# Attention probabilities turned by VectorE in blocks of 32 and by DMA through DRAM, in place of TensorE

## Chip, cores and metric

The kernel runs on one core of a Trainium2 chip. The time is that of the device for one execution, in microseconds (us). TensorE, VectorE (DVE), ScalarE (ACT), GpSimd (POOL) and SyncE (SP) are the core's engines; SyncE only issues transfers here.

## The reference

Two blocks run one after the other over 512 tokens of width 1024. The first (a pooling mixer and a gated recurrent mixer) is not touched by the change. The second has two layers, each with sliding-window attention beside a chunked gating branch:

```python
for l in range(DEPTH):                       # 2 layers
    h = x @ w_in[l] + b_in[l]
    q, k, v, z_a, u_g, v_g, z_g, g_a, g_g = split_columns(h)
    y_a = sliding_window_attention(q, k, v, sinks[l]) * silu(z_a)   # 8 query heads, 2 key heads, width 64
    y_g = chunked_spatial_gating(gelu(u_g), gelu(v_g), ...) * silu(z_g)
    merged = sigmoid(g_a) * (y_a @ w_branch_attn[l]) + sigmoid(g_g) * (y_g @ w_branch_gmlp[l])
    x = layer_norm(ALPHA * x + merged @ w_out[l] + b_out[l], ln_g[l], ln_b[l])
```

The attention works on blocks of 128 queries, each with the block of 128 keys before it and its own (256 keys), with a sink in the denominator:

```python
scores = q . k / 8 - slope * dist, masked to 0 <= dist < 128
m = max(scores, sink);  p = exp(scores - m);  denom = sum(p) + exp(sink - m)
out = (p / denom) @ v
```

## The kernel before

Products with weights are made in three terms (high x high, high x low, low x high) of float32 split into a high part, rounded, and a low one. Weights come from DRAM in loads of 1 MB (`load_chunk`, two buffers), each of which holds two pieces. The high part of a piece is made by ScalarE or, in the stretch of the attention, by a cast of VectorE (`c_split`, L2533), the low part by GpSimd (`split_lo`, L404). A load may be issued when the low part of the last piece in its buffer is done. A piece is split three units ahead of its use (`AHEAD = 3`).

TensorE runs through the units of a layer in a fixed order: q (4 units), k, v, za (4), u (4), vg (4 quarters), zg (4), ga (4), gg (4), then the branch products bra and brg, then a second half of these, then the output. A unit takes 24 products of 512 columns, some 6 us. Between the units stand small pieces of side work in an order that is written out by hand (`C_ORDER`): the attention is cut in 16 blocks, (pair of heads p, query block b) with p from 0 to 3 and b from 0 to 3, and one step of it follows each unit from za 1 on. With b = 0 there is no block of keys before, so half of the work falls away.

Step s on each engine, before the change:

- TensorE (`att_tensor`): for s = 6, 10, 14, 18 the products with the values of four blocks (one pair), into the second bank of `aux2`; then the scores of block s into `aux`; then the transpositions of the probabilities of block s - 2, two or four of 128x128, into the first bank of `aux2`.
- VectorE (`att_gate`, `att_vector`, `att_vector_out`): the gate of a pair when its products with the values are done; the scaling of the probabilities of block s - 1 (L2450); the mask and the row maximum of block s (L2460, L2465). After that it casts the next piece of weights.
- ScalarE (`att_scalar`): the copy of the turned probabilities of block s - 2 from PSUM to `pt` (four buffers, L1828), then the exponentials of block s (L1837), then the high part of a gated pair.

So step s = 7 follows the first quarter of vg, step 12 follows zg 1, step 15 ga 0, steps 16, 17 and 18 ga 1, 2 and 3. The gating branch's own side work (`mix`) follows gg 0 to gg 3. The branch products bra need all four gated pairs.

The first block of the model already turns an operand by VectorE's transposition in blocks of 32 (L2184) and a way through DRAM: SyncE writes `v_turn` (L950) and reads it back in four transfers (L958).

SyncE issues all weight loads of a layer in order, with nothing between them until two small loads near the layer's end. In a layer, load n holds pieces 2n and 2n + 1: load 7 and 8 are vg, 9 and 10 zg, 11 and 12 ga, 13 and 14 gg, 15 bra, 16 brg.

Of the kernel before, what the change touches and what calls it, by code (L numbers as in the profile page):

```python
# [28 lines left out]
F32 = mybir.dt.float32  # L29
F32R = mybir.dt.float32r  # L30
I32 = mybir.dt.int32
ALU = mybir.AluOpType
# [3 lines left out]
P = 128  # L36
# [3 lines left out]
SEQ = 512  # L40
# [97 lines left out]
def program(nc, a, out):  # L138
    with ExitStack() as ctx:
# [126 lines left out]
        with ExitStack() as before_g:  # L266
            ws = sb("ws", [P, 4, P], where=before_g)
            qs_b = sb("qs_b", [P, 4, SEQ], F32R, where=before_g)
            with ExitStack() as in_rows:
                brow = sb("brow", [P, D], where=in_rows)  # L270
            pt_more = [sb(f"pt{s}", [P, 4, P], where=before_g) for s in (2, 3)]
        gac = sb("gac", [P, 4, SEQ], where=in_c)
        ggc = sb("ggc", [P, 4, SEQ], where=in_c)

# [10 lines left out]
        with ExitStack() as before_m:  # L285
            kf = sb("kf", [P, SEQ], where=before_m)
            vf = sb("vf", [P, SEQ], where=before_m)
            vtc = sb("vtc", [P, CH, P], where=before_m)
            sc = [sb(f"sc{s}", [P, 2, 2 * P + 1], where=before_m) for s in range(2)]
            pr = [sb(f"pr{s}", [P, 2, 2 * P + 1], where=before_m) for s in range(2)]  # L290
            pt = [sb(f"pt{s}", [P, 4, P], where=before_m) for s in range(2)] + pt_more
            sgc = [xn[0][:, 0:SEQ], rstd[:, 0:SEQ]]
        with ExitStack() as after_m:
            mlo = sb("mlo", [P, KT, SEQ], F32R, where=after_m)
        in_c.close()
        qs = [(qs_a, qs_b)[n // 4][:, n % 4, :] for n in range(8)]
        qf = [s[:, :, :].rearrange("p x k -> p (x k)")[:, 0:SEQ] for s in sc]
        lng = sqs[:, :, :].rearrange("p s t -> p (s t)")[:, 0:D]
        lnb = xns[:, :, :].rearrange("p s t -> p (s t)")[:, 0:D]
# [55 lines left out]
        apt_full, apt_ready, ao_full = sem("apt_full"), sem("apt_ready"), sem("ao_full")  # L355
        ya_ready, yahi_ready, yalo_ready = sem("ya_ready"), sem("yahi_ready"), sem("yalo_ready")
        vgb_ready, vgg_ready, vgn, vgr_ready = (sem("vgb_ready"), sem("vgg_ready"), sem("vgn"),
                                                sem("vgr_ready"))
# [444 lines left out]
            return LC + C_STEPS * i  # L803

        ATT = [(p, b) for p in range(4) for b in range(CH)]
        STEP_OF = {}
        FREED = {}
        n_steps = 0
# [22 lines left out]
        def c_slots():  # L831

            att = 0
            order = []
            for entry in C_PLAN:
                stage, index, kind, m, half, u = entry
                for q in range(4 if kind == "vg" else 1):
                    side = []
                    if stage == "za" and index == 0:
                        side.append(("vtc", 0))  # L840
                        side.append(("ws", 0))
                    elif att < len(ATT) and stage in ("za", "u", "vg", "zg", "ga", "gg"):
                        side.append(("att", att))
                        att += 1
                    elif att < len(ATT) + 3 and att >= len(ATT):
                        side.append(("att", att))
                        att += 1
                    if stage in ("gg",) and index < 4:
                        side.append(("mix", index))
                    order.append((entry, q, side))  # L850
            return order
# [35 lines left out]
        def _(sp):  # L887
# [115 lines left out]
            for i in range(DEPTH):  # L1003
# [17 lines left out]
                for n, (kind, src) in enumerate(chunks):  # L1021
# [84 lines left out]
        def _(pe):  # L1106
# [272 lines left out]

            def att_tensor(i, s):  # L1380
                base = 16 * i
                for t in range(s - 6, s - 2) if s >= 6 and s % 4 == 2 else ():

                    p, b = ATT[t]
                    pe.wait_ge(apt_ready, 1 + base + t + 1)
                    if b == 0:
                        pe.wait_ge(ya_ready, 1 + 4 * i + p)
                    for kb_ in range(0 if b else 1, 2):
                        for x in range(2):
                            kv = (2 * p + x) // 4  # L1390
                            mm = pe.matmul(aux2[HD * x:HD * x + HD, 1, P * b:P * b + P],  # L1391
                                           vtc[:, b - 1 + kb_, HD * kv:HD * kv + HD],
                                           pt[t % 4][:, 2 * x + kb_, :],
                                           start=(kb_ == (0 if b else 1)), stop=(kb_ == 1))
                    mm.then_inc(ao_full, 1)
                if s < len(ATT):
# [16 lines left out]
                if 2 <= s < len(ATT) + 2:  # L1413

                    t = s - 2
                    b = ATT[t][1]
                    pe.wait_ge(aprob, 3 * (base + t) + 3)
                    pe.wait_ge(apt_ready, 1 + base + t)
                    for x in range(2):
                        for kb_ in range(0 if b else 1, 2):  # L1420
                            mm = pe.transpose(aux2[:, 0, P * (2 * x + kb_):P * (2 * x + kb_ + 1)],  # L1421
                                              pr[t % 2][:, x, P * kb_:P * kb_ + P], ident[:, :])
                    mm.then_inc(apt_full, 1)

            def side_tensor(i, what, n):
                if what == "vtc":
# [141 lines left out]

        @block.scalar
        def _(act):  # L1570
            act.sem_inc(apt_ready, 1)
# [245 lines left out]

            def att_scalar(i, s, between=None):
                base = 16 * i
                if 2 <= s < len(ATT) + 2:  # L1820
                    t = s - 2
                    z, first = t % 2, (0 if ATT[t][1] else 1)
                    act.wait_ge(apt_full, base + t + 1)
                    if t >= 4:
                        act.wait_ge(ao_full, base + t - 3)
                    if t == 2:
                        act.wait_ge(res_ready, 4 * i + 4)
                    act.activation(pt[t % 4][:, :, :].rearrange("p (x k) q -> p x k q", x=2)[:, :, first:, :],  # L1828
                                   aux2[:, 0, :].rearrange("p (x k q) -> p x k q", x=2, k=2)[:, :, first:, :],
                                   ACT.Copy).then_inc(apt_ready, 1)  # L1830
                if between is not None:
                    between()
                if s < len(ATT):
                    lo, z = (0 if ATT[s][1] else P), s % 2
                    act.wait_ge(arow, base + s + 1)
                    for x in range(2):
                        act.activation(pr[z][:, x, lo:], sc[z][:, x, lo:], ACT.Exp,  # L1837
                                       bias=sm[z][:, 0, x:x + 1], accum_out=sm[z][:, 1, x:x + 1])\
                           .then_inc(aexp, 1)
                if s >= 3 and ATT[s - 3][1] == CH - 1:  # L1840
                    p = ATT[s - 3][0]
                    act.wait_ge(ya_ready, 1 + 4 * i + p + 1)
                    act.activation(yah[:, p, :], sq[p % 2][:, 0:SEQ], ACT.Copy).then_inc(yahi_ready, 1)

            for i in range(DEPTH):
                def bias(col):
# [107 lines left out]
        def _(dve):  # L1954
# [486 lines left out]
            def att_vector(i, s):  # L2441
# [10 lines left out]
                if s < len(ATT):  # L2452
# [10 lines left out]
                    dve.wait_ge(asc_ready, 1 + 2 * (base + s) + 2)  # L2463
                    dve.wait_ge(sink_ready, 8 * i + 2 * p + min(b, 1) + 1)
                    dve.tensor_reduce(sm[z][:, 0, :], sc[z][:, :, lo:], AX_X, ALU.max, negate=True).then_inc(arow, 1)  # L2465

            def att_gate(i, s):
                if s >= 3 and ATT[s - 3][1] == CH - 1:
                    p = ATT[s - 3][0]
                    dve.wait_ge(ao_full, 16 * i + s - 2)  # L2470
                    dve.tensor_tensor(sq[p % 2][:, 0:SEQ], aux2[:, 1, :], za[:, p, :], ALU.mult)\
                       .then_inc(ya_ready, 1)

            def att_vector_out(i, s):
                if s >= 3 and ATT[s - 3][1] == CH - 1:
                    p = ATT[s - 3][0]
                    dve.wait_ge(yahi_ready, 4 * i + p + 1)
                    dve.tensor_tensor(yal[:, p, :], sq[p % 2][:, 0:SEQ], yah[:, p, :], ALU.subtract)\
                       .then_inc(yalo_ready, 1)

            def mix_vector(i, g):
# [194 lines left out]
```

## Time and profile before

| | |
|---|---|
| time, median of 3 runs | 1551.97 us (1551.46 to 1552.41) |
| the profiled execution | 1552.21 us, its span 1550.5 us |
| TensorE busy | 1540.2 us, 99% |
| VectorE busy | 1005.7 us, 65% |
| ScalarE busy | 592.1 us, 38% |
| GpSimd busy | 356.5 us, 23% |
| granted clock of TensorE, mean | 0.999 |
| moved by DMA | 149.78 MB, 97 GB/s |

A busy share is over the whole span; products of TensorE are pipelined, so that their durations overlap and the distance of their starts tells the pace. The attention of the first layer lies between 942 and 1062 us, that of the second between 1267 and 1387 us. A queue row (SPq) is an issue of a transfer; its time to landing is counted from the issue to the semaphore.

### The profile page before, as it was taken

How to read it: one execution, taken by the hardware profiler on the slowest of the kernel's cores; microseconds unless marked ns; L12 is line 12 of the kernel's file. 1: busy time of each engine (PE TensorE's matmuls, PEld its weight loads, DVE VectorE, ACT ScalarE, POOL GpSimd, SP SyncE). 2: the span in 40 equal slices, each digit the busy share in tenths (PEclk: the TensorE clock that was granted, in tenths of full speed). 3: DMA queues.
4: the chain of work that ended last, by engine and by line, in shares of the span. 5: the costliest groups of instructions: out<-in, count | busy, mean ns of one | idle time of the engine just before them, and what ended most of it. 6: DMA issues, size and time to landing. Idle time of an engine off the chain costs nothing.

```text
span 1550.5 us, 29971 instructions
## 1 busy us (share of the span) xinstructions
PE 1540.2 (99%) x12487; PEld 1381.8 (89%) x12487; DVE 1005.7 (65%) x1654; ACT 592.1 (38%) x1070; POOL 356.5 (23%) x333
## 2 busy tenths in 40 slices
PE   9999999999999999999999999999999999999998
PEld 9999999999999899899998898888888988888886
DVE  6656565775877678586786677567516786576346
ACT  5323232253444344334444445482112346541121
POOL 0000000020421214042142124334530043343510
PEclk9999999999999999999999999999999999999999
DMA  5322322323332523423243142222324322222331
GB/s 170 110 82 91 101 82 82 110 82 96 105 103 64 134 59 111 119 75 95 72 112 125 55 135 91 75 80 93 97 82 143 122 82 82 82 82 82 117 128 55
DMA packets 124722, 149.78 MB, mean 97 GB/s; under 512 B 4812, under 2 KB 100464, under 8 KB 124592
## 3 DMA queue, kind: packets, MB, share of 16 engines
q1 hardware_dynamic: 120880, 143.17, 30.1%
q10 hardware_dynamic: 3632, 4.53, 0.9%
q8 instruction: 100, 1.64, 0.4%
q0 software_dynamic: 80, 0.20, 0.1%
q14 instruction: 30, 0.25, 0.1%
HBM read 141.33 MB, written 6.55 MB: 95 GB/s over the span
## 4 chain that ended last, share of the span: by engine, by line
PE 98%; DVE 1%; DMA 0%; issue 0%; ACT 0%; SPq 0%; POOL 0%; ACTq 0%; DVEq 0%; POOLq 0%
PE acc L409 28%; PE acc L411 28%; PE acc L410 28%; PE aux L569 1%; PE aux L409 1%; PE aux L411 1%; PE aux L410 1%; PE aux L629 1%; PE aux L631 1%; PE aux L1391 1%; PE aux L1421 1%; PE aux L621 1%; PE aux L550 1%; PE aux L1410 1%; PE aux L1411 0%; PE aux L1445 0%
## 5 line engine op out<-in xcount | busy, mean ns | idle before, releaser
L409 PE MATMUL acc<-xhis,whi 128*128 128x264 f32 (+2 forms) x1848 | 611.3, 331 | 0.0
L411 PE MATMUL acc<-xhis,wlo 128*128 128x264 f32 (+2 forms) x1848 | 602.1, 326 | 0.0
L410 PE MATMUL acc<-xlos,whi 128*128 128x264 f32 (+2 forms) x1848 | 601.8, 326 | 0.0
L411 PEld LDWEIGHTS acc<-xhis,wlo 128*128 128x128 f32 x1848 | 347.9, 188 | 29.2
L409 PEld LDWEIGHTS acc<-xhis,whi 128*128 128x128 f32 x1848 | 348.0, 188 | 28.9 <-issue 0.3
L410 PEld LDWEIGHTS acc<-xlos,whi 128*128 128x128 f32 x1848 | 348.3, 188 | 26.8
L404 POOL TENSOR_TENSOR wlo<-raw,whi 128x1024 fp32r<-128x1024 f32 x84 | 207.7, 2473 | 377.0 <-DVE whi L2533 377.0
L400 ACT ACTIVATE whi<-raw 128x1024 fp32r<-128x1024 f32 x158 | 164.1, 1048 | 133.4 <-PE acc L411 119.2
L404 DVE TENSOR_TENSOR wlo<-raw,whi 128x1024 fp32r<-128x1024 f32 x81 | 99.8, 1235 | 36.9 <-ACT whi L400 36.7
L2230 DVE TENSOR_TENSOR wlo<-raw,whi 128x1024 fp32r<-128x1024 f32 x77 | 93.7, 1218 | 21.9 <-ACT whi L400 21.7
L2533 DVE CAST whi<-raw 128x1024 fp32r<-128x1024 f32 x84 | 66.8, 797 | 54.0 <-PE acc L411 53.8
L1082 POOL TENSOR_TENSOR kb<-kb,fb 128x264 f32<-128x264 f32 x16 | 17.3, 1100 | 285.9 <-PE aux L550 285.9
L1052 POOL TENSOR_TENSOR xns<-sqs 128x528 f32<-128x528 f32 x1 | 1.5, 1454 | 324.0 <-ACT sqs L1679 324.0
L409 PE MATMUL acc<-zhis,whi 128*128 128x264 f32 x256 | 73.2, 286 | 0.0
L411 PE MATMUL acc<-zhis,wlo 128*128 128x264 f32 x256 | 72.7, 284 | 0.0
L410 PE MATMUL acc<-zlos,whi 128*128 128x264 f32 x256 | 72.6, 284 | 0.0
L409 PEld LDWEIGHTS acc<-zhis,whi 128*128 128x128 f32 x256 | 48.2, 188 | 0.6
L410 PEld LDWEIGHTS acc<-zlos,whi 128*128 128x128 f32 x256 | 48.3, 189 | 0.0
L411 PEld LDWEIGHTS acc<-zhis,wlo 128*128 128x128 f32 x256 | 48.2, 188 | 0.0
L2134 DVE TENSOR_TENSOR h<-acc,h 128x528 f32<-128x528 f32 x32 | 22.6, 707 | 38.4 <-PE acc L411 38.4
L1072 POOL TENSOR_TENSOR tb<-tb 128x132 f32<-128x132 f32 (+5 forms) x96 | 38.9, 431 | 0.0
L1837 ACT ACTIVATE pr<-sc,sm 128x257 f32<-128x257 f32 (+1 forms) x64 | 30.4, 478 | 19.8 <-DVE sm L2465 19.7
(390 smaller groups left out, 2781.0 us busy)
## 6 DMA issues: line engine op xcount, KB each, us to landing
raw<-in_w_in SPq DMA_DIRECT2D x38, 1024.0 KB, 5.3
raw<-in_hgrn_w_in SPq DMA_DIRECT2D x32, 1024.0 KB, 6.4
raw<-in_pool_w_in SPq DMA_DIRECT2D x15, 1024.0 KB, 5.5
raw<-in_pool_w_out SPq DMA_DIRECT2D x8, 1024.0 KB, 5.1
raw<-in_hgrn_w_out SPq DMA_DIRECT2D x8, 1024.0 KB, 5.3
raw<-in_w_out SPq DMA_DIRECT2D x8, 1024.0 KB, 5.1
v_turn<-vb SPq DMA_DIRECT2D x8, 544.0 KB, 7.6
raw<-in_pool_w_grp SPq DMA_DIRECT2D x4, 1024.0 KB, 5.2
```

The costliest lines, as they stand in the source:

```text
L400: act.activation(piece(whi, kind, m), raw_view(kind, m), ACT.Copy).then_inc(hi_ready, 1)
L404: dve.tensor_tensor(piece(wlo, kind, m), raw_view(kind, m), piece(whi, kind, m), ALU.subtract).then_inc(lo_ready, 1)
L409: pe.matmul(dst, stat[0], mov[0], start=first, stop=False)
L410: pe.matmul(dst, stat[0], mov[1], start=False, stop=False)
L411: return pe.matmul(dst, stat[1], mov[0], start=False, stop=last)
L550: mm = pe.matmul(first_bank(c, x)[rows, :, col:col + 32], kb[par][x][:, META + t0:META + t0 + 32], both[:, :, t0:t0 + 32], start=True, sto ...
L1072: pool.tensor_tensor(tb[x][2 * m][:, 0:both.shape[1]], both[:, :, 0], both[:, :, 1], ALU.mult)\
L1082: pool.tensor_tensor(first_halves(dst, m), first_halves(src, m), both[:, :, 1].unsqueeze(2).to_broadcast([P, both.shape[1], m]), ALU.mult)\
L1837: act.activation(pr[z][:, x, lo:], sc[z][:, x, lo:], ACT.Exp, bias=sm[z][:, 0, x:x + 1], accum_out=sm[z][:, 1, x:x + 1])\
L2134: dve.tensor_tensor(halves(h[:, n, :]), acc_all(slot), halves(h[:, n, :]), ALU.add)\
L2230: dve.tensor_tensor(piece(wlo, kind, m), raw_view(kind, m), piece(whi, kind, m), ALU.subtract).then_inc(lo_ready, 1)
L2533: dve.tensor_copy(piece(whi, kind, M), raw_view(kind, M)).then_inc(hi_ready, 1)
```

## The change

The probabilities are no longer turned by TensorE and copied by ScalarE. In step t + 1, VectorE transposes the scaled probabilities of block t in blocks of 32x32, two instructions, into `pb` (two buffers, which lie in `sq[1]` and `xn[1]`). SyncE writes `pb` to a DRAM tensor `p_turn` (256 KB), and reads it back in four transfers of 32 partitions (64 KB each), which puts the blocks in their turned places, in `pt`. The places of these transfers among the weight loads in SyncE's order are given by numbers. The products with the values move from steps 6, 10, 14, 18 to 8, 12, 16, 19, and wait once a pair, for the transfers of all four blocks. The attention runs to step 19 (after gg 0). The gated pair is always in `sq[0]`. ScalarE's exponential waits for the transposition of the block two before.

```diff
+        VALUES_AT = {8: 0, 12: 1, 16: 2, 19: 3}
+        p_turn = nc.dram_tensor("p_turn", (len(ATT), P, SEQ), F32).ap()
...
-                    elif att < len(ATT) + 3 and att >= len(ATT):
+                    elif att <= max(VALUES_AT) and att >= len(ATT):
...
+                def probabilities_out(t):
+                    sp.wait_ge(pb_ready, 2 * (16 * i + t) + 2)
+                    sp.dma_start(p_turn[t], pb[t % 2].rearrange("p b n j -> p (b n j)")).then_inc(pb_sent[t % 2], 16)
+
+                def probabilities_in(t):
+                    sp.wait_ge(pb_sent[t % 2], 16 * ((16 * i + t) // 2) + 16)
+                    if t == 2:
+                        sp.wait_ge(res_ready, 4 * i + 4)
+                    if 16 * i + t >= 4:
+                        sp.wait_ge(ao_full, 16 * i + 4 * (t // 4))
+                    blocks = p_turn[t].rearrange("(a p) n -> p a n", a=4)
+                    for b in range(4):
+                        sp.dma_start(pt[t % 4][32 * b:32 * b + 32, :, :, :].rearrange("p a n j -> p a (n j)"),
+                                     blocks[:, :, P * b:P * b + P]).then_inc(pt_landed, 16)
+
+                queue = [(2 * n - 12.5, "load", n) for n in range(len(chunks))]
+                queue += [(t + 2.5, "out", t) for t in range(len(ATT))]
+                queue += [(max(t + 3.3, 4 * (t // 4) + 4.3 + 0.1 * (t % 4) if t >= 4 else 0), "in", t)
+                          for t in range(len(ATT))]
+                for _, what, n in sorted(queue):
...
-                for t in range(s - 6, s - 2) if s >= 6 and s % 4 == 2 else ():
+                for t in range(4 * VALUES_AT[s], 4 * VALUES_AT[s] + 4) if s in VALUES_AT else ():
-                    pe.wait_ge(apt_ready, 1 + base + t + 1)
+                    if b == 0:
+                        pe.wait_ge(pt_landed, 64 * (base + t + 4))
...
-                    for x in range(2):
-                        for kb_ in range(0 if b else 1, 2):
-                            mm = pe.transpose(aux2[:, 0, P * (2 * x + kb_):P * (2 * x + kb_ + 1)],
-                                              pr[t % 2][:, x, P * kb_:P * kb_ + P], ident[:, :])
-                    mm.then_inc(apt_full, 1)
...
-                    act.activation(pt[t % 4][:, :, :].rearrange("p (x k) q -> p x k q", x=2)[:, :, first:, :],
-                                   aux2[:, 0, :].rearrange("p (x k q) -> p x k q", x=2, k=2)[:, :, first:, :],
-                                   ACT.Copy).then_inc(apt_ready, 1)
...
+                    if base + s >= 2:
+                        act.wait_ge(pb_ready, 2 * (base + s - 1))
...
+                if 1 <= s < len(ATT) + 1:
+                    t = s - 1
+                    first, z = (0 if ATT[t][1] else 1), t % 2
+                    dve.wait_ge(aprob, 3 * (base + t) + 3)
+                    if base + t >= 2:
+                        dve.wait_ge(pb_sent[z], 16 * ((base + t) // 2))
+                    for x in range(2):
+                        dve.transpose(pb[z][:, :, 2 * x + first:2 * x + 2, :].rearrange("p b k j -> p k b j"),
+                                      pr[z][:, x, P * first:2 * P].rearrange("p (k b j) -> p k b j", b=4, j=32))\
+                           .then_inc(pb_ready, 1)
...
-                if s >= 3 and ATT[s - 3][1] == CH - 1:
-                    p = ATT[s - 3][0]
-                    dve.wait_ge(ao_full, 16 * i + s - 2)
-                    dve.tensor_tensor(sq[p % 2][:, 0:SEQ], aux2[:, 1, :], za[:, p, :], ALU.mult)\
+                if s in VALUES_AT:
+                    p = VALUES_AT[s]
+                    dve.wait_ge(ao_full, 16 * i + 4 * p + 4)
+                    if 4 * i + p:
+                        dve.wait_ge(yahi_ready, 4 * i + p)
+                        dve.wait_ge(yalo_ready, 4 * i + p)
+                    dve.tensor_tensor(sq[0][:, 0:SEQ], aux2[:, 1, :], za[:, p, :], ALU.mult)\
```

Sorted, the order of SyncE's queue around the ends of the four pairs is: load 8, write 1, read 1, write 2, read 2, load 9, write 3, read 3, write 4; load 10, write 5, reads 4 and 5, write 6, read 6, load 11, write 7, read 7, write 8; load 12, write 9, reads 8 and 9, write 10, read 10, load 13, write 11, read 11, write 12; load 14, write 13, reads 12 and 13, write 14, read 14, load 15, write 15, read 15; load 16. A "read" is the four transfers of one block.

## Rows read from the trace of the kernel before

**Rows 1.** The page's chain that ended last, shares of the span by engine

```profile
PE 98%; DVE 1%; DMA 0%; issue 0%; ACT 0%; SPq 0%; POOL 0%; ACTq 0%; DVEq 0%; POOLq 0%
```

**Rows 2.** Timeline of TensorE around step 9: start us, us, engine, line, operation

```profile
1001.04 0.60 PE L1421 MATMUL aux<-ident,pr 128*128 128x128 f32 x4
...
1001.39 0.48 PE L409 MATMUL acc<-whi,xhis 128*128 128x512 f32 x1
...
1001.71 0.39 PE L410 MATMUL acc<-wlo,xhis 128*128 128x512 f32 x1
...
1001.94 0.40 PE L411 MATMUL acc<-whi,xlos 128*128 128x512 f32 x1
```

**Rows 3.** Timeline of TensorE, attention work at steps 6, 8, 12, 16 and 19

```profile
979.88 1.75 PE L1391 MATMUL aux<-pt,vtc 128*64 128x128 f32 x28
...
994.22 0.22 PE L1410 MATMUL aux<-kch,qs_b 128*128 128x128 f32 x1
...
1021.38 0.22 PE L1410 MATMUL aux<-kch,qs_b 128*128 128x128 f32 x1
...
1048.55 0.60 PE L1421 MATMUL aux<-ident,pr 128*128 128x128 f32 x4
...
1067.72 1.05 PE L1445 MATMUL aux<-wst,vn 128*128 128x128 f32 x8
```

**Rows 4.** Timeline of SyncE's queue, loads 8, 9, 11, 13 and 15

```profile
966.40 0.37 SPq L873 DMA_DIRECT2D raw<-in_w_in  x1
...
978.73 0.37 SPq L873 DMA_DIRECT2D raw<-in_w_in  x1
...
1005.87 0.37 SPq L873 DMA_DIRECT2D raw<-in_w_in  x1
...
1037.45 0.37 SPq L873 DMA_DIRECT2D raw<-in_w_in  x1
...
1060.27 0.37 SPq L873 DMA_DIRECT2D raw<-in_w_branch_attn  x1
```

**Rows 5.** SyncE's waits in 930 to 1090: us in total, times, longest

```profile
SPq L381 <- POOL wlo L404: 154.0, 13, 18.4
```

**Rows 6.** Transfers: issues, KB each, median us to landing (all; then single windows)

```profile
raw<-in_w_in SPq DMA_DIRECT2D x38, 1024.0 KB, 5.3
...
out<-xr SPq DMA_DIRECT2D x2, 256.0 KB, 2.0
...
raw<-in_hgrn_w_in SPq DMA_DIRECT2D x1, 1024.0 KB, 6.5
...
v_turn<-vb SPq DMA_DIRECT2D x1, 544.0 KB, 7.4
...
v_turn<-vb SPq DMA_DIRECT2D x1, 544.0 KB, 3.0
...
vts<-v_turn SPq DMA_DIRECT2D x1, 128.0 KB, 3.3
```

**Rows 7.** Timeline of SyncE's queue: a load, a write behind it, four reads

```profile
384.57 0.37 SPq L873 DMA_DIRECT2D raw<-in_hgrn_w_in  x1
...
384.99 0.57 SPq L950 DMA_DIRECT2D v_turn<-vb  x1
...
829.40 2.79 SPq L958 DMA_DIRECT2D vts<-v_turn  x4
```

**Rows 8.** VectorE: the block transposition, and the scaling of block 15

```profile
L2184 DVE STREAM_TRANSPOSE vb<-ib x16: 700/702/708, 376.1 to 825.5; 128x512 f32<-128x512 f32 x16
...
1048.03 2.13 DVE L2450 TENSOR_SCALAR pr<-pr,sm 128x256 f32<-128x256 f32 x2
```

**Rows 9.** Windows at the end: PE, PEld, DVE, ACT, POOL busy, PEclk, DMA share

```profile
1543.00:1544.00 1.00, 0.44 (x4) 0.24 (x2) 0.57 (x3) 0.00 (x0) 0.00 (x0) 1.00 0.89 369
...
1546.00:1547.00 1.00, 0.00 (x0) 0.00 (x0) 1.00 (x2) 0.00 (x0) 0.00 (x0) 0.73 0.00 0
```

**Rows 10.** Timeline of TensorE, its opening

```profile
0.99 6.27 PE L1110 MATMUL aux<-ones_d 128*128 128x128 f32 x28 [0.99 <-POOL ones_d L1043]
```

More of the change, by code:

```diff
@@ L270, in program @@
                 brow = sb("brow", [P, D], where=in_rows)
-            pt_more = [sb(f"pt{s}", [P, 4, P], where=before_g) for s in (2, 3)]
+            pt_more = [sb(f"pt{s}", [P, 4, 4, 32], where=before_g) for s in (2, 3)]
         gac = sb("gac", [P, 4, SEQ], where=in_c)
@@ L290, in program @@
             pr = [sb(f"pr{s}", [P, 2, 2 * P + 1], where=before_m) for s in range(2)]
-            pt = [sb(f"pt{s}", [P, 4, P], where=before_m) for s in range(2)] + pt_more
+            pt = [sb(f"pt{s}", [P, 4, 4, 32], where=before_m) for s in range(2)] + pt_more
             sgc = [xn[0][:, 0:SEQ], rstd[:, 0:SEQ]]
@@ L296, in program @@
         qs = [(qs_a, qs_b)[n // 4][:, n % 4, :] for n in range(8)]
+        pb = [rows[:, 0:SEQ].rearrange("p (b n j) -> p b n j", b=4, n=4) for rows in (sq[1], xn[1])]
         qf = [s[:, :, :].rearrange("p x k -> p (x k)")[:, 0:SEQ] for s in sc]
@@ L354, in program @@
         aexp, aprob, sink_ready = sem("aexp"), sem("aprob"), sem("sink_ready")
-        apt_full, apt_ready, ao_full = sem("apt_full"), sem("apt_ready"), sem("ao_full")
+        pb_ready, pb_sent = sem("pb_ready"), [sem(f"pb_sent{n}") for n in range(2)]
+        pt_landed = sem("pt_landed")
+        ao_full = sem("ao_full")
         ya_ready, yahi_ready, yalo_ready = sem("ya_ready"), sem("yahi_ready"), sem("yalo_ready")
@@ L1020, in _ @@
                         chunks.append(("vg", w_out_c[:, 8 * i + 4 * c:8 * i + 4 * c + 4, 512 * j:512 * j + 512]))
-                for n, (kind, src) in enumerate(chunks):
+                def probabilities_out(t):
[16 more added lines that the diff above has]
+                for _, what, n in sorted(queue):
+                    if what == "out":
+                        probabilities_out(n)
+                        continue
+                    if what == "in":
+                        probabilities_in(n)
+                        continue
+                    kind, src = chunks[n]
                     N = C_PIECES // 2 * i + n
@@ L1392, in att_tensor @@
                                            vtc[:, b - 1 + kb_, HD * kv:HD * kv + HD],
-                                           pt[t % 4][:, 2 * x + kb_, :],
+                                           pt[t % 4][:, :, 2 * x + kb_, :],
                                            start=(kb_ == (0 if b else 1)), stop=(kb_ == 1))
@@ L1412, in att_tensor @@
                     mm.then_inc(asc_full, 1)
[L1413 to L1418, printed above, removed]
-                    for x in range(2):
-                        for kb_ in range(0 if b else 1, 2):
-                            mm = pe.transpose(aux2[:, 0, P * (2 * x + kb_):P * (2 * x + kb_ + 1)],
-                                              pr[t % 2][:, x, P * kb_:P * kb_ + P], ident[:, :])
-                    mm.then_inc(apt_full, 1)
             def side_tensor(i, what, n):
@@ L1570, in _ @@
         def _(act):
-            act.sem_inc(apt_ready, 1)
             act.sem_inc(on_ready, 1)
@@ L1819, in att_scalar @@
                 base = 16 * i
[L1820 to L1827, printed above, removed]
-                    act.activation(pt[t % 4][:, :, :].rearrange("p (x k) q -> p x k q", x=2)[:, :, first:, :],
-                                   aux2[:, 0, :].rearrange("p (x k q) -> p x k q", x=2, k=2)[:, :, first:, :],
-                                   ACT.Copy).then_inc(apt_ready, 1)
                 if between is not None:
@@ L1839, in att_scalar @@
                            .then_inc(aexp, 1)
-                if s >= 3 and ATT[s - 3][1] == CH - 1:
-                    p = ATT[s - 3][0]
+                if s in VALUES_AT:
+                    p = VALUES_AT[s]
                     act.wait_ge(ya_ready, 1 + 4 * i + p + 1)
-                    act.activation(yah[:, p, :], sq[p % 2][:, 0:SEQ], ACT.Copy).then_inc(yahi_ready, 1)
+                    act.activation(yah[:, p, :], sq[0][:, 0:SEQ], ACT.Copy).then_inc(yahi_ready, 1)
             for i in range(DEPTH):
@@ L2465, in att_vector @@
                     dve.tensor_reduce(sm[z][:, 0, :], sc[z][:, :, lo:], AX_X, ALU.max, negate=True).then_inc(arow, 1)
-            def att_gate(i, s):
-                if s >= 3 and ATT[s - 3][1] == CH - 1:
-                    p = ATT[s - 3][0]
-                    dve.wait_ge(ao_full, 16 * i + s - 2)
-                    dve.tensor_tensor(sq[p % 2][:, 0:SEQ], aux2[:, 1, :], za[:, p, :], ALU.mult)\
+                if 1 <= s < len(ATT) + 1:
[8 more added lines that the diff above has]
+                           .then_inc(pb_ready, 1)
+            def att_gate(i, s):
+                if s in VALUES_AT:
+                    p = VALUES_AT[s]
+                    dve.wait_ge(ao_full, 16 * i + 4 * p + 4)
[3 more added lines that the diff above has]
+                    dve.tensor_tensor(sq[0][:, 0:SEQ], aux2[:, 1, :], za[:, p, :], ALU.mult)\
                        .then_inc(ya_ready, 1)
             def att_vector_out(i, s):
-                if s >= 3 and ATT[s - 3][1] == CH - 1:
-                    p = ATT[s - 3][0]
+                if s in VALUES_AT:
+                    p = VALUES_AT[s]
                     dve.wait_ge(yahi_ready, 4 * i + p + 1)
-                    dve.tensor_tensor(yal[:, p, :], sq[p % 2][:, 0:SEQ], yah[:, p, :], ALU.subtract)\
+                    dve.tensor_tensor(yal[:, p, :], sq[0][:, 0:SEQ], yah[:, p, :], ALU.subtract)\
                        .then_inc(yalo_ready, 1)
```

## The prediction

> **What bounds the kernel now.** I read the chain of waits first. TensorE holds 98% of the chain that ends last [rows 1], so whatever leaves TensorE's stream shortens the run, and whatever makes TensorE wait lengthens it by the same amount. The other engines matter only where TensorE waits for them. Next I read TensorE's timeline around one attention step [rows 2] for the pace, then the starts of the attention work at the steps that the change touches [rows 3], then SyncE's issue times of the weight loads [rows 4] and what SyncE waits for [rows 5], last the landings of transfers [rows 6] and how fast SyncE can issue them [rows 7]. The first layer is used throughout; the second shows the same work at the same distances, so each term counts twice.
>
> **What leaves TensorE.** Per layer 12 of the 16 attention steps have four transpositions and 4 (those with b = 0) have two. In the timeline four transpositions start at 1001.04, the next product at 1001.39 and the one behind at 1001.71; two products otherwise start 0.23 apart [rows 2]. Without the four, the product would start at 1001.04 and the next at 1001.27: 0.44 us saved, 0.11 for each. Over both layers 24 x 0.44 + 8 x 0.22 = 12.3 us. The recorded duration of 0.27 each would give 112 x 0.27 = 30 us, but the durations overlap; the starts decide. The Trainium skill (VectorE: DVE Perf Modes, The three transpose paths) gives 390 ns for one TensorE transposition of a 128x128 bf16 block and 311 ns for VectorE's blocks of 32; by it, 112 transpositions would be 43.7 us, and the sum below 1536. The starts in the rows say 0.11, and the measured row is what I use.
>
> **What is added on VectorE and taken from ScalarE.** Two block transpositions a step, of 256 elements a partition. One of 512 takes 0.70 us [rows 8], so I take 0.37 each and 0.75 a step (below: half of 0.70 each; above: 0.70 each, 1.4 a step). They stand behind the row maximum, so they delay neither the exponential nor the softmax chain, but they do delay the cast of a weight piece that follows, and by it POOL's low part and the next load: 0.75 us later. That is not on TensorE's path: a piece is cast three units, about 19 us, ahead of its use. ScalarE loses 32 copies out of PSUM; it is not what TensorE waits for, so nothing comes of it. The new waits of the exponential on the turned block and of the gate on the earlier split are for work one step or several old, and cost nothing.
>
> **What is moved to SyncE and the transfer queue.** For each step there is a write of 256 KB and four reads of 64 KB, all on the queue that loads the weights, in a fixed order. The order puts the last block of each head pair as follows: block 3 behind load 9, block 7 behind load 11, block 11 behind load 13, block 15 behind load 15 (the first branch weights). SyncE waits only for POOL's low parts today [rows 5], so those loads go out the moment a buffer is free: 978.73, 1005.87, 1037.45, 1060.27 [rows 4]. The probabilities are then long ready: block 15 is scaled by 1050.2 [rows 8], turned by 1051, but its write must wait for load 15. TensorE now takes each pair's products with the values in one go and waits for the last block of the four. So what counts is the time from the issue of that load to the landing of the last read:
>
> issue of the load, 0.4 (384.57 to 384.99, [rows 7]); the write behind a 1 MB load. A 544 KB write issued 0.42 behind such a load landed after 7.4, the load after 6.5, so the write landed 1.3 behind the load; alone it took 3.0, and a 256 KB write 2.0 [rows 6]. A load alone lands after 5.3. For 256 KB that is between 5.2 and 7.4 from its issue; I take 6.0. Then SyncE issues four reads: between 4 x 0.42 = 1.7 and 2.8 [rows 7], taken 2.2. The last read lands after 2.0 to 3.3 [rows 6], taken 2.6 for 64 KB. Sum 0.4 + 6.0 + 2.2 + 2.6 = 11.2 us (9.3 to 13.9).
>
> Now how long TensorE gives it. The arrival at a step is today's start, less the transpositions saved so far (0.44 or 0.22 each), less 1.8 for the pair's own 28 records of value products, which today stand two steps (for the last pair one) earlier, as at 979.88 [rows 3]. Step s comes after the transpositions of blocks 0 to s - 3; loads 9, 11, 13 and 15 hang on VectorE's steps 5, 9, 13 and 17, thus on blocks 0 to 2, 6, 10 and 14: 1.1, 2.6, 4.2 and 5.7 saved, plus the 0.75 of VectorE.
> - First pair, step 8: arrival 994.22 - 1.8 - 2.2 = 990.2. Load 9: 978.73 - 1.1 + 0.75 = 978.4. But SyncE is held: after load 8 (966.40, now 966.5) it does a write (0.4 + 6.0), reads (2.2), a second write that lands alone (2.7) and its reads (2.2): 13.5 in 11.9, so load 9 is 1.6 late. Left 10.2, wait 1.0.
> - Second pair, step 12: arrival 1021.38 - 1.8 - 3.8 = 1015.8, load 11 at 1005.87 - 2.6 + 0.75 = 1004.0. Left 11.8: no wait.
> - Third pair, step 16: arrival 1048.55 - 1.8 - 5.3 = 1041.5, load 13 at 1037.45 - 4.2 + 0.75 = 1034.0. Left 7.5, wait 3.7.
> - Last pair, step 19: arrival 1067.72 - 1.8 - 6.2 = 1059.8, load 15 at 1060.27 - 5.7 + 0.75 = 1055.3. Left 4.5, wait 6.7.
>
> An earlier wait moves both load and arrival, so they add: 11.4 a layer, 22.8 in all. Behind a waiting TensorE stand VectorE's gate, then the cast and ScalarE's split; they restart with it and have three units of lead, so I add nothing.
>
> **Clock.** At the end of the kernel TensorE stops at 1543.44, and the granted clock is 1.00 until inside the stretch from 1546 to 1547, whose mean is 0.73 [rows 9]: it falls from 2.4 to 1.2 GHz some 3.0 us after the last product. A wait of 6.7 us will see that, one of 3.7 just. On the way back: the opening's 28 records took 6.27 us [rows 10], 0.22 apart, twice the 0.11 of a transposition's record, so half pace can last 6 us and cost at most 3; below, nothing. I take the middle, 1.5 for each long wait and half for the 3.7: 2 x 2.25 = 4.5.
>
> **Sum.** The profiled execution took 1552.2 (span 1550.5), 0.2 above the median. 1552.2 - 12.3 + 22.8 + 4.5 = 1567.2; for a median, 1567.0.
>
> **Slack of the loads.** Load 11 lands near 1011, and its piece is cast about step 12 (1021.38), so a load may be some 10 us late [rows 3, 4, 6]. The worst delay I find is 2 to 4 us. Thus no weight is late.
>
> **Rivals.**
> - The write is not held behind the load, since the 16 engines share their time: it lands after 2.6. Then the chain is 7.8, the waits 0.3 and 3.3, and the time 1552.2 - 12.3 + 7.2 = 1547.1, faster. The 7.4 against 3.0 of the same write [rows 6] speaks against it. It decides from a chain under 9.1, where the two waits (9.1 - 7.5 and 9.1 - 4.5) equal the 6.2 saved. 8 in 100.
> - All costs at their short ends: a chain of 9.3, waits 1.8 and 4.8, no clock lost: 1553.1, no measurable change. 7 in 100.
> - A load falls behind by more than its 10 us, since SyncE waits for writes while a weight is due: TensorE then waits for weights also in the u and vg units. Such a miss of 4 us a layer would give 1575 and more. 4 in 100.
> - The transpositions give back their whole recorded duration: 1552.2 - 30 + 27.3 = 1549.5. The starts speak against it. 1 in 100. The 390 ns of the Trainium skill (VectorE: DVE Perf Modes, The three transpose paths) would lie further the same way.
> - The forecast: 80 in 100.
>
> **Numbers.** The forecast's own range goes from 1556 to 1581: at the top a chain of 12.7 (waits 2.5, 0.9, 5.2, 8.2) and 7.5 for the clock. With the all-short case the range is 1553 to 1581. A measurement of this kernel tells 0.2% (3.1 us) from no change. Faster: the first and fourth rival and a little of the second, 0.10; same 0.05; slower 0.85.
>
> **What the profile after will show.** No transposition from the probabilities on TensorE; some 64 block transpositions of about 0.37 us on VectorE; TensorE's value products waiting for a transfer, most at the last pair, next at the third, hardly at the second; SyncE waiting for its own writes about 6 us behind loads 9, 11, 13, 15; the granted clock below 1.00 just after the last pair's wait. It would be wrong if the writes behind a load land in 3 us, or if the order of the queue lets a load slip by 10 us.

## The result, and the profile after

The changed kernel takes 1609.03 us, median of 4 runs (1607.99 to 1609.83), against 1551.72 us of the kernel before, measured with it: a ratio of 1.0368, 95% interval 1.035 to 1.0386. It is slower by 57 us. Slower was forecast with 0.85, but the size was not: 1609 lies 28 us above the range's upper end.

The head of the page, and its chain by engine:

```profile
span 1607.4 us, 29978 instructions
...
PE 80%; DVE 7%; DMA 6%; issue 3%; POOL 2%; ACT 1%; SPq 1%; DVEq 0%; ACTq 0%; POOLq 0%
```

TensorE held 98% of the chain before [rows 1]; now the other engines, the transfers and the issues hold 20% of it. What TensorE waited for, over the whole run (us in total, times, longest):

```profile
PE aux L1423 <- DMA pt<-p_turn: 17.5, 3, 9.0
PE acc L412 <- POOL wlo L407: 11.4, 2, 5.9
PE aux L1442 <- DVE sc L2471: 9.2, 5, 4.7
PE acc L412 <- ACT ug L1906: 6.4, 2, 3.2
PE acc L412 <- DVE vn L2574: 4.3, 2, 2.2
```

Only the first row is the wait that the prediction priced: the products with the values (L1423), for the last read. The other four, 31 us together, are waits for the scores of the step before to be drained (L1442), for a weight's low part, and for accumulators to be drained by ScalarE (`ug`) or VectorE (`vn`): for VectorE and what follows it. None of them is in the prediction. The page's costliest groups name what VectorE itself waited for:

```profile
L2484 DVE STREAM_TRANSPOSE xns<-pr 128x256 f32<-128x256 f32 x32 | 12.3, 423 | 65.5 <-DMA p_turn<-xns 65.5
```

65.5 us over both layers, in front of the block transpositions into `xns`, the second of the two buffers, for the writes out of that buffer. One round of it in the first layer, as SyncE's queue shows it:

```profile
1014.81 0.40 SPq L878 DMA_DIRECT2D raw<-in_w_in  x1
1015.25 0.77 SPq L1028 DMA_DIRECT2D p_turn<-xns  x1
1021.16 1.74 SPq L1038 DMA_DIRECT2D pt<-p_turn  x4
1022.94 0.43 SPq L1028 DMA_DIRECT2D p_turn<-sqs  x1
1030.67 0.40 SPq L878 DMA_DIRECT2D raw<-in_w_in  x1
```

and the landings of the first layer, from 930 to 1120 (issues, KB each, median us to landing):

```profile
raw<-in_w_in SPq DMA_DIRECT2D x11, 1024.0 KB, 5.6
...
p_turn<-sqs SPq DMA_DIRECT2D x8, 256.0 KB, 2.2
p_turn<-xns SPq DMA_DIRECT2D x8, 256.0 KB, 5.9
```

and the timeline of VectorE, then of GpSimd (POOL), in the same time:

```profile
1016.08 0.69 DVE L2476 TENSOR_REDUCE sm<-sc 128x2 f32<-128x514 f32 x1
1021.24 0.77 DVE L2484 STREAM_TRANSPOSE xns<-pr 128x256 f32<-128x256 f32 x2 [4.47 <-DMA p_turn<-xns]
1021.93 0.65 DVE L2557 CAST whi<-raw 128x1024 fp32r<-128x1024 f32 x1
...
1027.46 0.65 DVE L2557 CAST whi<-raw 128x1024 fp32r<-128x1024 f32 x1
```

```profile
1028.19 2.39 POOL L407 TENSOR_TENSOR wlo<-raw,whi 128x1024 fp32r<-128x1024 f32 x1 [3.12 <-DVE whi L2557]
```

Read together: block 7 was turned by 1006.1, but in SyncE's order its write stands behind load 11, which goes out only at 1014.81; the write follows at 1015.25, 9.1 us after its data were ready. From the second buffer, it then lands some 6 us later. VectorE has the row maximum of block 10 done at 1016.8, and next must turn block 9 into the same buffer. It waits 4.5 us, until 1021.24. Behind the transposition stands the cast of a weight piece, at 1021.93. The next step's cast, at 1027.46, feeds the low part for which load 12 waits, at 1030.67; behind load 12 stands write 9, for which VectorE waits with block 11. The waits of the odd blocks 3 to 15 form a ring: write behind the load, transposition behind the write, the next step's cast behind the transposition, low part behind that cast, load behind the low part. One turn takes 15.9 us (1014.81 to 1030.67): 0.4 to the write, 6.0 to the transposition, 0.7 to the first cast, 5.5 of VectorE's next step, 0.7 to the low part, 2.5 to the next load. It covers two steps of the attention, for which TensorE needs some 12.5 where nothing holds it (in experiment 5, 118.8 us for 19 steps). Writes out of the first buffer have, but for block 0, no load right in front; they land in 2.2 us, and no even block waits.

TensorE does not have to wait for the ring to come round. Behind VectorE's first wait (4.9 us, until 974.08), ScalarE and then TensorE show:

```profile
979.66 0.51 ACT L1848 ACTIVATE pr<-sc,sm 128x257 f32<-128x257 f32 x1 [3.46 <-DVE sm L2476]
...
982.07 0.69 ACT L1906 ACTIVATE ug<-acc,vec 128x512 f32<-128x512 f32 x1
```

```profile
982.90 0.54 PE L412 MATMUL acc<-whi,xhis 128*128 128x512 f32 x1 [3.20 <-ACT ug L1906]
```

VectorE's next row maximum is late, ScalarE's exponential waits for it, ScalarE's drain of a u unit stands behind the exponential, and TensorE waits for that drain.

By the starts in the trace, from the scores of step 0 to the first products of the gating branch's side work, a layer's stretch took 125.0 us before (942.71 to 1067.72, [rows 3]) and 152.2 after (942.97 to 1095.16), 27.2 longer.

The wait of the last pair, which was forecast, is in the run too, and with it the clock. TensorE's timeline, then windows (busy of PE, PEld, DVE, ACT, POOL, then PEclk, DMA share, GB/s):

```profile
1075.89 0.77 PE L412 MATMUL acc<-xhis,whi 128*128 128x512 f32 x1 [5.51 <-POOL wlo L407]
...
1091.98 3.26 PE L1423 MATMUL aux<-pt,vtc 128*64 128x128 f32 x28 [9.03 <-DMA pt<-p_turn]
```

```profile
1082.00:1092.00 10.00, 0.97 (x7) 0.47 (x5) 1.21 (x2) 0.69 (x1) 2.40 (x2) 0.68 0.50 158
1086.00:1087.00 1.00, 0.00 (x0) 0.00 (x0) 0.00 (x0) 0.00 (x0) 0.00 (x0) 0.50 1.06 410
...
1092.00:1096.00 4.00, 4.00 (x32) 3.67 (x33) 0.72 (x2) 0.00 (x0) 0.00 (x0) 0.53 0.00 0
```

TensorE stood 9.0 us; in 1086 to 1087 the granted clock is 0.50, half of full speed, and the 28 records behind the wait took 3.26 us in place of 1.75 [rows 3]. At the other pairs the value products wait hardly at all: a TensorE that is late everywhere gives the reads their time.

The low clock came behind shorter waits too. Behind the wait for `ug` above (3.2 us), a wait for `vn` (2.2 us) and one for scores (3.2 us), which ended at 982.90, 1013.5 and 1043.7, the windows show:

```profile
984.00:986.00 2.00, 2.00 (x6) 1.51 (x6) 0.80 (x2) 1.16 (x5) 0.00 (x0) 0.50 0.73 130
1015.00:1017.00 2.00, 2.00 (x6) 1.54 (x6) 1.73 (x5) 1.98 (x4) 0.00 (x0) 0.50 0.42 68
1045.00:1047.00 2.00, 2.00 (x7) 1.52 (x5) 0.36 (x1) 1.97 (x5) 1.56 (x1) 0.50 0.01 4
```

What this costs can be worked out against experiment 5, in which TensorE has the same work. The spans are 1607.4 and 1542.4 us, 65.0 apart; TensorE's waits add up to 52.0 and 5.8 us, 46.2 apart. The other 18.8 us are the same work done more slowly, at a mean granted clock of 0.983 in place of 0.999. So the clock took some 19 us, an estimate.

### The profile page after: what moved, and what is told of

It reads as the page before. It is cut to its first block, busy times and chain, and to the rows that moved or that the text cites. A ratio compares the mean times of both kernels' runs of the same rounds, so it can differ in the third digit from the quotient of the medians.

```text
span 1607.4 us, 29978 instructions
## 1 busy us (share of the span) xinstructions
PE 1548.5 (96%) x12375; PEld 1382.9 (86%) x12375; DVE 1045.2 (65%) x1718; ACT 576.8 (36%) x1038; POOL 357.5 (22%) x333
## 4 chain that ended last, share of the span: by engine, by line
PE 80%; DVE 7%; DMA 6%; issue 3%; POOL 2%; ACT 1%; SPq 1%; DVEq 0%; ACTq 0%; POOLq 0%
PE acc L412 23%; PE acc L414 23%; PE acc L413 23%; DMA p_turn<-xns 6%; POOL wlo L407 2%; DVE pr L2461 1%; PE aux L572 1%; PE aux L412 1%; PE aux L414 1%; PE aux L413 1%; DVE whi L2557 1%; PE aux L632 1%; PE aux L634 1%; DVE sc L2471 1%; PE aux L624 1%
## 5 line engine op out<-in xcount | busy, mean ns | idle before, releaser
L412 PE MATMUL acc<-xhis,whi 128*128 128x264 f32 (+2 forms) x1848 | 613.3, 332 | 15.7 <-POOL wlo L407 11.4
L412 PEld LDWEIGHTS acc<-xhis,whi 128*128 128x128 f32 x1848 | 350.2, 190 | 46.4 <-issue 12.5
L2557 DVE CAST whi<-raw 128x1024 fp32r<-128x1024 f32 x84 | 61.4, 732 | 54.0 <-PE acc L414 53.9
L412 PE MATMUL acc<-zhis,whi 128*128 128x264 f32 x256 | 73.3, 286 | 0.0
L2484 DVE STREAM_TRANSPOSE xns<-pr 128x256 f32<-128x256 f32 x32 | 12.3, 423 | 65.5 <-DMA p_turn<-xns 65.5
L2461 DVE TENSOR_SCALAR pr<-pr,sm 128x256 f32<-128x256 f32 (+1 forms) x64 | 54.2, 887 | 1.1
L412 PEld LDWEIGHTS acc<-zhis,whi 128*128 128x128 f32 x256 | 48.1, 188 | 0.7 <-DVE zlos L2157 0.2
```

The costliest lines, as they stand in the source:

```text
L412: pe.matmul(dst, stat[0], mov[0], start=first, stop=False)
L2461: dve.tensor_scalar(pr[z][:, x, lo:2 * P], pr[z][:, x, lo:2 * P], sm[z][:, 2, x:x + 1], None, ALU.mult).then_inc(aprob, 1)
L2557: dve.tensor_copy(piece(whi, kind, M), raw_view(kind, M)).then_inc(hi_ready, 1)
```

## The experiments

Eight kernels, one of them run twice, in three groups; each group had the kernel before beside it (median 1552.09, 1552.12 and 1551.82). Each is the changed kernel with an edit, except the third, which is the kernel before with one.

**1. The writes ahead of the loads.** Only the ties in the order are turned: a write and a load with the same number change places (and, by rounding, write 14 comes ahead of the reads of block 13):

```diff
-                queue += [(t + 2.5, "out", t) for t in range(len(ATT))]
+                queue += [(t + 2.4, "out", t) for t in range(len(ATT))]
```

> The changed kernel with each block's write placed ahead of the weight load that it stood behind; the rest of SyncE's order as it was. Theory A (VectorE's transposition of block t waits until the write of block t - 2 has landed, and that write stands behind a 1 MB load): the write lands some 2 us after its issue instead of 6, VectorE's waits of 3.6 to 6.0 us go, and so do TensorE's waits for scores, weights and the accumulators; the last read lands some 4 us sooner too. Time 1540 to 1550, below the kernel before. Rival B (VectorE has too much work, with its transpositions and the scalings held up by GpSimd): its waits go but its steps stay longer than TensorE's, and the time stays above 1585. Rival C (the transfers as such slow the weight loads): above 1585 too, with loads that land late.

Measured: 1554.61 us (10 runs, 1552.61 to 1555.38), ratio 1.0013 (1.0003 to 1.0022). Moving one write in front of one load in every second step takes 54 of the 57 us away. Theories B and C fall: VectorE has the same work, and the transfers move the same bytes. Not every write lands early now; those of the even blocks go out 2.4 to 5.6 us behind a load, with reads between, and their median in the first layer is

```profile
p_turn<-sqs SPq DMA_DIRECT2D x8, 256.0 KB, 4.7
```

Yet VectorE waits for writes 0.3 us in the whole run. So a late landing alone is not enough to cost the time; in the changed kernel the write was also issued late, 9.1 us in the round above, since SyncE stood at a load that could not go out yet. No run takes the two apart further.

The forecast of 1540 to 1550 was missed, though; the end of the last pair shows what is left, SyncE first, then TensorE:

```profile
1055.66 0.43 SPq L1028 DMA_DIRECT2D p_turn<-xns  x1
1058.20 0.40 SPq L878 DMA_DIRECT2D raw<-in_w_branch_attn  x1
1059.01 1.74 SPq L1038 DMA_DIRECT2D pt<-p_turn  x4
```

```profile
1064.80 3.26 PE L1423 MATMUL aux<-pt,vtc 128*64 128x128 f32 x28 [3.61 <-DMA pt<-p_turn]
```

Write 15 is ahead of the load now, but its reads are not: they were issued at 1059.01, 0.8 us behind the load, and TensorE got them 5.8 us later, after a wait of 3.6 and at the low clock (3.26 us again). Twice (3.6 + 1.5) is 10 of the 12 us that leaving out the transpositions gave.

**2. Four buffers in place of two.** The order stays as in the change. The two further buffers lie in `kf` and `vf`, which hold nothing at that time:

```diff
-        pb = [... for rows in (sq[1], xn[1])]
+        pb = [... for rows in (sq[1], xn[1], kf, vf)]
...
-                    if base + t >= 2:
-                        dve.wait_ge(pb_sent[z], 16 * ((base + t) // 2))
+                    if base + t >= 4:
+                        dve.wait_ge(pb_sent[t % 4], 16 * ((base + t) // 4))
```

> The changed kernel with four buffers for the turned blocks instead of two (the further two in tiles that are free by then), SyncE's order unchanged. Theory A: VectorE's wait for the write before last goes, since it now waits for the write four blocks back; what stays is the wait of the value products for the last read behind a load, which the prediction priced. With the chain as measured in the changed kernel (9.8 us from load 15 to the products, in place of 11.2) the waits are 2.3 and 5.3 a layer, so 1552 - 12.3 + 15.2 + about 3 for the clock: 1558, range 1552 to 1567. Rival B or C: above 1585.

Measured: 1562.73 us (1562.20 to 1563.94), ratio 1.0071 (1.0054 to 1.0087). The writes still stand behind the loads and VectorE does not wait for them: 46 us are gone. This run is the case that the prediction worked out, without the wait that it left out, and it lies 4 us below the forecast of 1567 (and in the range of 1552 to 1567 given before this run, 5 us above its 1558). TensorE's waits, its timeline, and SyncE's around load 15:

```profile
PE aux L1423 <- DMA pt<-p_turn: 14.7, 4, 7.1
PE acc L412 <- DVE vn L2574: 1.8, 2, 0.9
...
PE acc L412 <- ACT ug L1906: 0.8, 2, 0.4
```

```profile
1043.35 1.75 PE L1423 MATMUL aux<-pt,vtc 128*64 128x128 f32 x28 [0.45 <-DMA pt<-p_turn]
```

```profile
1068.78 3.25 PE L1423 MATMUL aux<-pt,vtc 128*64 128x128 f32 x28 [7.09 <-DMA pt<-p_turn]
```

```profile
1056.98 1.73 SPq L1038 DMA_DIRECT2D pt<-p_turn  x4
1058.85 0.40 SPq L878 DMA_DIRECT2D raw<-in_w_branch_attn  x1
1059.28 0.51 SPq L1028 DMA_DIRECT2D p_turn<-vf  x1
1065.52 1.74 SPq L1038 DMA_DIRECT2D pt<-p_turn  x4
```

From load 15 to the products 9.9 us passed (1058.85 to 1068.78); 6.2 for the write (1059.28 to 1065.52), 1.7 for the issues, 1.5 for the last read.

**3. The kernel before without the transpositions**, but for the first four blocks of the first layer:

```diff
                     pe.wait_ge(apt_ready, 1 + base + t)
+                    if base + t >= 4:
+                        pe.sem_inc(apt_full, 1)
+                        return
```

> The kernel before, in which TensorE turns the first four blocks of the first layer alone and leaves out the other transpositions (the copies read what stands in PSUM). It measures what the removal of the transpositions is worth by itself. By the starts in the trace 0.44 us for four and 0.22 for two: 112 less 14 transpositions give 10.8 us, so 1541. If the recorded durations counted (0.27 each), 1525.

Measured: 1540.56 us (1540.17 to 1543.16), ratio 0.993 (0.9913 to 0.9947): 11.5 us for 98 transpositions, 0.118 each. Reading the starts, not the durations, was right. For all 112 it is 13.2 us, an estimate of the most that the change could win by them.

**4. Both edits together** (1 and 2).

> Both edits together: four buffers, and the writes ahead of the loads. Theory A: within 2 us of the writes ahead alone, since a write that lands after 2 us holds nobody with two buffers either. If it is faster by more, the second buffer pair still hides a wait.

Measured: 1554.81 us (1551.91 to 1555.75), ratio 1.0015 (1.0005 to 1.0024), as with the first edit alone. Buffers and order are two ways around the same wait, and with the order right the buffers add nothing.

**5. Another order of the queue.** Each block's write and reads stand right behind its transposition, ahead of the next load; for blocks whose `pt` buffer is still in use, right behind the value products that free it:

```diff
-                queue += [(t + 2.5, "out", t) for t in range(len(ATT))]
-                queue += [(max(t + 3.3, 4 * (t // 4) + 4.3 + 0.1 * (t % 4) if t >= 4 else 0), "in", t)
+                queue += [(t + 1.3, "out", t) for t in range(len(ATT))]
+                queue += [(max(t + 1.4, 4 * (t // 4) + 4.35 + 0.01 * (t % 4) if t >= 4 else 0), "in", t)
                           for t in range(len(ATT))]
```

> The changed kernel with another order of SyncE alone: the write of block t and its reads right after VectorE has turned it, ahead of the next load (for blocks whose buffer is still read by a value product, right behind that product). The products with the values stay at steps 8, 12, 16, 19. Theory A (only the place in the order cost time): no wait of TensorE for a read is left, VectorE waits for no write, the two 3.6 us waits and the slow clock behind them, 10 us in the run with the writes ahead, are gone: 1542 to 1546. Rival D (reads ahead of loads hold the loads up, and TensorE waits for weights): 1550 or more, with waits of TensorE for low parts.

Measured: 1544.33 us (5 runs, 1543.38 to 1546.10), ratio 0.995 (0.9937 to 0.9964): below both kernels, 0.5% under the one before. Writes that happen to follow a load still land late (median 3.7 us for the odd blocks), but VectorE waits for none. TensorE's waits, and its timeline at the last pair:

```profile
PE acc L412 <- DVE vn L2574: 1.8, 2, 0.9
...
PE acc L412 <- ACT ug L1906: 0.8, 2, 0.4
```

```profile
1061.61 1.75 PE L1423 MATMUL aux<-pt,vtc 128*64 128x128 f32 x28
```

No wait for a read is left, and the 28 records take 1.75 us. The layer's stretch is 120.5 us (942.78 to 1063.28), 4.5 below the kernel before where the transpositions alone make 6.2; most of the rest is the two waits above, 1.3 us a layer. The first stands where the moved value products stood; why ScalarE's `ug` is 0.4 late was not looked into. The same kernel was run again in the third group:

> The fastest run's kernel once more, beside the one with the mixed places on the same chip: 1543 to 1546 again.

It gave 1544.01 us (1543.30 to 1544.07), ratio 0.9949 (0.9936 to 0.9963).

**6. The same order with the value products at their old steps:**

```diff
-        VALUES_AT = {8: 0, 12: 1, 16: 2, 19: 3}
+        VALUES_AT = {6: 0, 10: 1, 14: 2, 18: 3}
```

(and the reads of blocks 4 and up two steps earlier with them).

> As before, but the products with the values back at steps 6, 10, 14, 18, where the kernel before has them. Theory A: the last write of a pair lands one step after its block is turned, so the earlier place costs no wait: 1540 to 1545, the same as with the later places or 1 to 2 us faster, since the gate of the last pair no longer meets the gating branch's first side work. Rival E (the way through DRAM needs the later places): TensorE waits for reads at these steps and the time is some us above the other.

Measured: 1549.40 us (11 runs, 1547.11 to 1552.69), ratio 0.9988 (0.9979 to 0.9997), above the 1540 to 1545 of theory A. Rival E holds: TensorE waits for reads six times, in the first layer 1.0 us at step 6, 1.0 at step 14 and 1.6 at step 18. The later places in the change are worth 5 us. The wait for the vg accumulators (L412 behind VectorE's `vn`) is gone in this run.

**7. The writes on ScalarE's queue**, SyncE's order otherwise unchanged:

```diff
+                if 2 <= s < len(ATT) + 2:
+                    act.wait_ge(pb_ready, 2 * (base + s - 1))
+                    act.dma_start(p_turn[s - 2], pb[s % 2]...).then_inc(pb_sent[s % 2], 16)
```

> The changed kernel, in which ScalarE issues the writes on its own queue (at the head of its step t + 2, behind the wait for the turned block that it has anyway), while SyncE issues loads and reads in the unchanged order. It asks why a write behind a load takes 6 us. If the queue holds it (first in, first out), the writes land in 2 to 3 us, VectorE does not wait, and the time is that of the writes ahead, 1550 to 1558, or up to 5 us more because the last block is written a step later. If the engines' shared time holds it, the writes that meet a load still take 5 to 6 us and the time is 1560 to 1600.

Measured: 1553.72 us (10 runs, 1552.39 to 1555.28), ratio 1.0008 (0.9999 to 1.0018). The time is the one expected of a queue that holds its writes, the landings are not. The write of block 4 was issued 0.44 us behind load 9, on the other queue:

```profile
978.55 0.40 SPq L878 DMA_DIRECT2D raw<-in_w_in  x1
...
978.99 0.36 ACTq L1841 DMA_DIRECT2D p_turn<-sqs  x1
```

```profile
raw<-in_w_in SPq DMA_DIRECT2D x1, 1024.0 KB, 6.5
p_turn<-sqs ACTq DMA_DIRECT2D x1, 256.0 KB, 5.5
```

It took 5.5 us, while one issued at 985.55 with no load under way took 2.0. So in this case another queue did not carry a write past a load that had just been issued. What helped seems to be the moment: ScalarE issues a step after the transposition whatever SyncE waits for, and mostly with no load under way, as the medians of 2.2 and 2.9 us of its writes in the first layer say. That is argued from the landings and fits the late landings of experiment 1, which cost nothing; no run tells it apart by itself.

**8. Mixed places**, with the order of 5: the value products at steps 7, 10, 15 and 19.

> The order of the queue as in the run that was fastest, with the products with the values at steps 7, 10, 15, 19. At step 10 they stand again in front of the wait for VectorE's drain of the vg accumulators (0.9 us a layer in the fastest run, none where the products stood at step 10), and at 7 and 15 they are one step behind the places at which they waited 1.0 us for a read. If the 0.9 us was cover that the moved products took away, the time is 1541.5 to 1543.5, 1 to 2.5 us below the fastest run. If the reads wait again at step 10 it is 1544 to 1547.

Measured: 1544.28 us (1543.18 to 1545.23), ratio 0.9953 (0.9939 to 0.9966): no better than 5.

```profile
PE aux L1423 <- DMA pt<-p_turn: 2.2, 2, 1.2
...
PE acc L412 <- ACT ug L1906: 0.8, 2, 0.4
```

The wait for `vn` is gone, so the value products at step 10 did cover it, but a read is waited for instead, 1.1 us a layer. The trade is even. The profiled stretch of a layer is 0.2 us shorter (942.57 to 1062.86), which the times can't tell.

## Why the prediction was wrong

**The step that failed** is the part on VectorE: it priced the block transpositions by their duration and named, of the new waits, only those of ScalarE's exponential and of the gate. The diff has a third, in front of each transposition, for the write two blocks before to have left the buffer. The prediction knew that such a write stands behind a 1 MB load and lands after 6 us, and used it for the reads alone; it never asked who else waits for the same semaphore. Worked out in its own terms: write 7 behind load 11 lands near 1004.0 + 0.4 + 6.0 = 1010.4; VectorE must turn block 9 behind the row maximum of step 10, which ended at 1012.3 in the kernel before and would end some 5 us sooner with what was saved and moved, near 1007: a wait of 3 us, seven times a layer, and each one puts off the next load. The measured row has 32.8 us a layer (65.5 for both), 4.7 each. Experiments 1 and 2 both remove this wait, each another way, and bring 54 and 46 us back.

In numbers, the miss against 1567.0 is 42 us. The four waits of TensorE that were left out are 31, the clock took 14 more than its 4.5 (below), and the waits for the last read, 17.5 in place of 22.8, take 5 off: 40.

**And the slack was misread.** The sentence that the transpositions delay neither the exponential nor the softmax chain holds for their own step, not for the next: a wait of 4.9 us in front of them reached TensorE by the next row maximum, exponential and drain (3.2 us, ended at 982.90). And the sentence that the cast has three units of lead and costs nothing holds for 0.75 us, but not for a delay that comes back every second step, since the next load, and by it the next write, wait for the low part behind a later cast. Each turn of the ring then starts later, until TensorE waits for a low part as well (5.5 us, ended at 1075.89).

**What leaves TensorE**, 12.3 us: right; 11.5 measured for 98 of the 112.

**The transfers.** 6.0 for the write behind a load: measured 5.9, 6.1, 6.2. Four issues in 2.2: 1.74. The last read 2.6: 1.5 to 1.9. The chain of 11.2 was 9.9. With VectorE's wait out of the way (experiment 2) TensorE's waits were 0, 0, 0.45 and 7.1 a layer, in place of 1.0, 0, 3.7 and 6.7; their sum is 7.5, not 11.4. At the third pair the chain was 1.5 shorter (9.7) and TensorE came 1.4 later than worked out (1042.9), 1.3 of it from the two small waits in experiment 2's rows. At the last pair three errors cancel: the chain was 1.3 shorter and TensorE 1.4 later, but load 15 went out 3.1 later (1058.85; forecast 1055.3 and the 0.45 of the third pair), since SyncE was still issuing the reads of block 14, from 1056.98 to 1058.71. That 7.1 came out so near to 6.7 is luck. The hold was worked out in the prediction for load 9 and left out for load 15.

**The clock.** 1.5 for a long wait: right, 3.26 against 1.75 us; the 0.75 for the third pair did not come, since its wait was 0.45 us (experiment 2: 1.75 us for its 28 records). But the term of 4.5 in all counted two waits a layer. In the changed kernel the clock was halved behind five waits of the first layer, the shortest 2.2 us, and took some 19 us in all, the second largest part of the miss.

**A small term that was left out:** the value products were moved away from step 10, where their 1.75 us stood in front of a wait for VectorE's drain; 0.9 us a layer, shown by experiments 5, 6 and 8.

**The rivals.** None of them had this mechanism. The one in which a load slips and TensorE waits for weights comes nearest in what TensorE sees, but its cause was another and its chance 4 in 100. The one in which the writes are not held behind the loads was rightly given little: at the last pair, on which the forecast stood, the write landed after 6.1 and 6.2 us, and the median of the odd blocks is 5.9. The one in which the transpositions give back their whole recorded duration falls with experiment 3.

**What the profile was to show.** The 64 block transpositions, the waits of the last pair, SyncE's waits of 6 us and the low clock are all there. The wait "next at the third pair" is not.

## What to carry to other kernels

List every wait that an edit adds, with its engine, and for a buffer that is sent away ask when it is issued and when it lands: a transfer that stands in a queue behind a load which itself waits is as late as that load, and with two buffers the engine that fills them is late with it. Where a queue's own order closes a ring (transfer, engine, weight piece, load, transfer), a delay is paid every turn, whatever lead a single piece has. Put small transfers that somebody waits for ahead of large ones that nobody needs yet. Moving a transfer in the order was worth 54 us here, a second pair of buffers 46, and both together no more than the first.

## What the runs showed that I had not expected

- A 256 KB write issued 0.44 us behind a 1 MB load took 5.5 us on another queue than the load's, 5.9 us at the median on the same one, and 2.0 to 2.2 us with no load under way. The load took 6.5 us beside it; the loads of the kernel before took 5.3 at the median.
- VectorE's scaling of probabilities (two instructions, 0.62 us) took up to 2.78 us in stretches in which GpSimd made a low part (2.77 from 1055.82, with GpSimd's from 1055.79); no block transposition of the attention ran beside a low part, so whether it would be slowed as well stays open. A block transposition of 256 elements took 0.42 us (0.402 to 0.447 over 32 of them), more than the 0.37 that I took; two in a row took 0.77, close to my 0.75.
